# Window attention of a two-block model: the copies of turned probability tiles divided between ScalarE and VectorE by the parity of the unit

## The reference

```python
def softmax_with_sink(s, sink):
    m = jnp.maximum(jnp.max(s, axis=-1, keepdims=True), sink)
    p = jnp.exp(s - m)
    return p / (jnp.sum(p, axis=-1, keepdims=True) + jnp.exp(sink - m))
...
        p = softmax_with_sink(jnp.concatenate([s_lat, s_ctx], axis=-1), sink_f).astype(v.dtype)
        o = jnp.einsum('bhgqk,bkhd->bqhgd', p[..., :3 * BLOCK], vblk)
        return o + jnp.einsum('bhgqc,bchd->bqhgd', p[..., 3 * BLOCK:], vc)
```

## Time and profile before

| what | us |
|---|---|
| median of 3 runs | 2783.05 (2780.53 to 2784.03) |
| the profiled execution, its own time | 2781.07 |
| its span in the profile | 2779.2 |
| TensorE matmul busy in the span | 2627.3 |
| VectorE busy | 1275.1 |
| ScalarE busy | 651.1 |

### The profile page before, as it was taken

How to read it: one execution, slowest core, us unless ns; L and a number is a source line. 1 busy time by engine, 2 the same in 40 slices (tenths; PEclk the granted TensorE clock), 3 DMA queues, 4 the chain that set the end, 5 groups by cost and what they waited for, 6 DMA issues and landing times.

```text
span 2779.2 us, 38625 instructions
## 1 busy us (share of the span) xinstructions
PE 2627.3 (95%) x14448; PEld 2112.1 (76%) x14448; DVE 1275.1 (46%) x1893; ACT 651.1 (23%) x1222; POOL 1355.4 (49%) x880
## 2 busy tenths in 40 slices
PE   7989999999999989889989999999899999899997
PEld 6667777777777767656768888888788887688886
DVE  6941222253222235445454444444486666555555
ACT  2220000031000013567230000000165553211112
POOL 6365555545555563133536344444343425776661
PEclk9999999999999999999989999999999999999998
DMA  5124444434444441100111111111111111222221
GB/s 188 52 77 159 144 143 145 144 113 139 151 146 148 151 137 54 39 1 1 39 39 61 61 60 60 60 58 59 51 37 40 45 46 36 79 91 98 92 97 53
DMA packets 67372, 235.61 MB, mean 85 GB/s; under 512 B 8144, under 2 KB 9552, under 8 KB 67152
## 3 DMA queue, kind: packets, MB, share of 16 engines
q1 hardware_dynamic: 65792, 233.64, 25.5%
q10 hardware_dynamic: 1488, 0.69, 0.1%
HBM read 232.21 MB, written 2.10 MB: 84 GB/s over the span
## 4 chain that ended last, share of the span: by engine, by line
PE 84%; DVE 8%; issue 3%; ACT 2%; POOL 1%; DMA 1%; DVEq 0%; SPq 0%; ACTq 0%; POOLq 0%
PE ps L650 66%; PE ps L1160 2%; PE ps L1183 2%; PE ps L1048 2%; PE ps L843 2%; PE ps L805 2%; PE ps L1122 1%; PE ps L1034 1%; DVE X L2142 1%; PE ps L769 1%; PE ps L1114 1%; DVE Alo L1734 1%; PE ps L683 1%; DVE tmp L1727 1%; DVE X L1745 1%
## 5 line engine op out<-in xcount | busy, mean ns | idle before, releaser
L501 POOL TENSOR_SCALAR whi<-raw 128x1024 fp32r<-128x1024 f32 x332 | 365.6, 1101 | 1060.3 <-DMA raw<-in_stream 1060.0
L503 POOL TENSOR_TENSOR wlo<-raw,whi 128x1024 fp32r<-128x1024 f32 x332 | 808.9, 2437 | 27.7
L650 PE MATMUL ps<-Ahi,whi 128*128 128x512 f32 (+1 forms) x2128 | 730.7, 375 | 39.9 <-DVE Alo L1734 19.3
L650 PE MATMUL ps<-Alo,whi 128*128 128x512 f32 (+1 forms) x2128 | 720.7, 370 | 0.0
L650 PE MATMUL ps<-Ahi,wlo 128*128 128x512 f32 (+1 forms) x2128 | 719.4, 369 | 0.0
L650 PEld LDWEIGHTS ps<-Ahi,whi 128*128 128x128 f32 x2128 | 376.5, 191 | 131.2 <-issue 21.4
L650 PEld LDWEIGHTS ps<-Ahi,wlo 128*128 128x128 f32 x2128 | 375.7, 190 | 68.9
L650 PEld LDWEIGHTS ps<-Alo,whi 128*128 128x128 f32 x2128 | 376.6, 191 | 66.4 <-issue 0.7
L650 PE MATMUL ps<-hhi,whi 128*128 128x512 f32 x1120 | 373.3, 370 | 19.7 <-DVE X L2142 18.6
L650 PE MATMUL ps<-hhi,wlo 128*128 128x512 f32 x1120 | 373.4, 370 | 0.0
L650 PE MATMUL ps<-hlo,whi 128*128 128x512 f32 x1120 | 370.7, 368 | 0.0
(11 more groups left out here) (291 smaller groups left out, 2782.0 us busy)
## 6 DMA issues: line engine op xcount, KB each, us to landing
raw<-in_stream SPq DMA_DIRECT2D x428, 512.0 KB, 3.8
X<-in_xT SPq DMA_DIRECT2D x2, 1024.0 KB, 6.3
arena<-in_dft SPq DMA_DIRECT2D x1, 2048.0 KB, 16.7
out_xT<-X SPq DMA_DIRECT2D x2, 1024.0 KB, 4.3
X<-in_ctxT SPq DMA_DIRECT2D x1, 1024.0 KB, 19.1
w<-in_stream SPq DMA_DIRECT2D x2, 512.0 KB, 4.3
vec<-in_vec SPq DMA_DIRECT2D x1, 364.5 KB, 7.4
arena<-in_fmap SPq DMA_DIRECT2D x1, 256.0 KB, 12.3
```

Of the source, the lines that this page charges most:

```text
L501: pool.tensor_scalar(whi[:, s, part], raw[:, s, part], 1.0, 1.0, ALU.mult, ALU.mult).then_inc(sem("w_hi"), 1)
L503: pool.tensor_tensor(wlo[:, s, part], raw[:, s, part], whi[:, s, part], ALU.subtract).then_inc(sem("w_split"), 1)
L650: mm = pe.matmul(dst[c], w[:, b % RING, off:off + P], rhs(k, part, c0, n), start=(k == 0 and w is whi and part == 0), stop=(k == kn - 1 an ...
```

## The change

`take_turned` is now on two engines. ScalarE copies the turned tiles of even units, VectorE those of odd units, in a function of the same shape. In VectorE's loop the copy stands behind the reciprocal and ahead of `take_values`. The one semaphore `ptA` becomes `ptA0` and `ptA1`, one for each parity, and TensorE's three waits on it are rewritten: ahead of the first turned tile on the copy of the unit two before, ahead of the fifth tile on the copy of the unit one before, and ahead of part 0 of the values on both.

```diff
--- before.py
+++ after.py
@@ -1027,10 +1027,11 @@
 
                 ks = keys(UNITS[u][2])
                 pe.wait_ge(*when("pA", u + 1))
-                pe.wait_ge(*when("ptA", u + 1))
+                if u >= 2:
+                    pe.wait_ge(*when(f"ptA{u % 2}", u // 2))
                 for t in range(len(ks)):
-                    if t == 4:
-                        pe.wait_ge(*when("ptA", u + 2))
+                    if t == 4 and u:
+                        pe.wait_ge(*when(f"ptA{(u - 1) % 2}", (u - 1) // 2 + 1))
                     mm = pe.transpose(turned(u, t), probA[u % 4][:, 1 + t * P:1 + (t + 1) * P], ident[:, :])
                 mm.then_inc(sem("turnA"), 1)
 
@@ -1039,7 +1040,8 @@
                 g, _, n, _ = UNITS[4 * four]
                 ks = keys(n)
                 if part == 0:
-                    pe.wait_ge(*when("ptA", 4 * four + 6))
+                    for parity in range(2):
+                        pe.wait_ge(*when(f"ptA{parity}", 2 * four + 2))
                     pe.wait_ge(*when("oA", four + 1))
                 for t in range(len(ks)):
                     if t // 2 == part:
@@ -1518,7 +1520,6 @@
                 take_query(0, 0, h)
 
 
-            act.sem_inc(sem("ptA"), 2)
             act.sem_inc(sem("sA_free"), 2)
             def take_turned(u):
 
@@ -1531,10 +1532,10 @@
                     copy(ptA[u // 4 % 2][:, 4, h * P:(h + 1) * P], psf[:, 7 * 512:7 * 512 + P])
                     nk = 4
                 copy(ptA[u // 4 % 2][:, 0:nk, h * P:(h + 1) * P],
-                     psf[:, four:four + nk * P].rearrange("p (t q) -> p t q", t=nk)).then_inc(sem("ptA"), 1)
+                     psf[:, four:four + nk * P].rearrange("p (t q) -> p t q", t=nk)).then_inc(sem("ptA0"), 1)
 
             for u in range(N_UNITS + LEAD):
-                if u >= LEAD:
+                if u >= LEAD and (u - LEAD) % 2 == 0:
                     take_turned(u - LEAD)
                 if u < N_UNITS:
                     n = UNITS[u][2]
@@ -2079,6 +2080,19 @@
                 move(O[:, 4 * g + 2 * e:4 * g + 2 * e + 2, n * P:(n + 1) * P],
                      ps[:, 6, 0:2 * P].rearrange("p (a q) -> p a q", a=2)).then_inc(sem("oA"), 1)
 
+            def take_turned(u):
+
+                n, h = UNITS[u][2:]
+                nk = len(keys(n))
+                four = (4 + u % 2) * 512
+                dve.wait_ge(*when("turnA", u + 5))
+                dve.wait_ge(*when("oA_done", u // 4 + 1))
+                if nk > 4:
+                    dve.tensor_copy(ptA[u // 4 % 2][:, 4, h * P:(h + 1) * P], psf[:, 7 * 512:7 * 512 + P])
+                    nk = 4
+                dve.tensor_copy(ptA[u // 4 % 2][:, 0:nk, h * P:(h + 1) * P],
+                     psf[:, four:four + nk * P].rearrange("p (t q) -> p t q", t=nk)).then_inc(sem("ptA1"), 1)
+
             for u in range(N_UNITS + LEAD + 4):
                 if u < N_UNITS:
                     n = UNITS[u][2]
@@ -2095,6 +2109,8 @@
                     c = sm[:, (u - 1) % 8, :]
                     dve.wait_ge(*when("sA_free", u + 2))
                     dve.reciprocal(c[:, 2:3], c[:, 1:2]).then_inc(sem("denA"), 1)
+                if LEAD <= u < N_UNITS + LEAD and (u - LEAD) % 2:
+                    take_turned(u - LEAD)
                 four, part = divmod(u - LEAD - 7, 4)
                 if four >= 0 and part == 0:
                     take_values(four)
```

## The result

The changed kernel takes 2787.65 us (median of 14 runs, 2784.97 to 2791.81), the kernel before 2780.69 in the runs made beside it (14 runs, 2776.84 to 2784.03). The ratio is 1.0027, with a 95% interval from 1.0019 to 1.0035: 5.3 to 9.7 us slower. The time lies in the range and 0.6 us from the forecast; but the forecast stood on a median of before of 2783.05, so the step of 5.1 us was 7.0 in truth. That the two errors, 1.9 us too small a step and a starting point 2.4 us too high, nearly cancel in the time is luck. The likeliest case, a difference too small to tell, was not the one that came: nearly all of the interval is slower by over 0.2%.

A forecast was written before the change was run, and what follows sets the result against it. TensorE was taken to bound the kernel, so only its waits inside the attention count. Late values 4.8 plus fifth tile 0.3 made 5.1 us on 2781.07, plus 1.98 to the median: 2788.2 us, range 2781 to 2792 (8 in 10).

The forecast's parts named there:

- The likeliest case: Whole kernel: a difference from no change within about 0.2%, 5.6 us; chance 0.55, against slower 0.40 and faster 0.05.
- Nothing won on ScalarE's side: TensorE's nine short waits behind exponentials: fewer ScalarE copies gain 0, at most 0.2 us; in four the row maximum was last.
- The rival of relief: ScalarE's halved queue removes short waits if the taking is early enough; at most 3.9 us faster, 2779.2 us; chance 0.18.
- Late values, 4.8 us: Turns that leave 2: VectorE's copy stands ahead of the taking of values, so TensorE's values start late, 4.8 us in all.
- the step from the end of the taking to the values: From VectorE's taking to TensorE's values: 0.05 us for the semaphore, read from ScalarE's copy (1250.11 to 1250.16).
- The fifth tile, 0.3 us in two turns: Turns 17 and 64: the fifth tile, sharing bank 7, waits for VectorE's late copy, about 0.17 us each, together 0.3.
- Row maxima priced at nothing: VectorE's row maxima of odd units come up to 0.8 us later behind the copies; cost to the exponentials priced at 0.
- The seven stalls unchanged: TensorE's seven stalls ended by GpSimd's scaling, 12.0 us in all, behind splittings, were taken as staying unchanged.
- The sum, 5.1 us: Whole kernel: late values 4.8 plus fifth tile 0.3, all else 0, gives 5.1 us slower, with bounds 3.8 to 7.1.
- The signs: Profile after: values of turns 23, 27, 51, 59, 75, 99 wait behind the taking; new row 3 to 5 us, 15 to 19 times.
- signs of being wrong: Stage shorter, VectorE copies under 0.5 us, exponential waits over 1 us longer, or a low clock stretch coming or going.
- The clock as a rival: New 0.38 us gaps behind the stalls of turns 23 and 71 bring low clock stretches, 3.4 us more, 2791.6 us; chance 0.15.

The follow-up runs named there:

- e3_threes: The changed kernel, but VectorE copies only units that leave 3 when divided by 4 (24 of 96), ScalarE all others; 2788.40 us, ratio 1.0017 to before.
- e9: The changed kernel, but ScalarE takes the values out of PSUM, ahead of the exponential; odd units' copies stay on VectorE; 2784.55 us, ratio 1.0016 to before.
- e2_ones: The changed kernel, but VectorE copies only units that leave 1 when divided by 4 (24 of 96), ScalarE all others; 2780.32 us, ratio 1.0000 to before.
- e1_swap: The changed kernel, but VectorE takes the values first and copies the odd unit behind that; 2791.25 us, ratio 1.0041 to before.
- e4: The changed kernel with parities exchanged: VectorE copies even units right behind its row maximum, ahead of the query splitting, ScalarE odd ones; 2774.49 us, ratio 0.9982 to before.
- e7: VectorE order: row maximum, reciprocal, copy of an even unit, splitting, taking of values; ScalarE copies odd units; 2770.17 us, ratio 0.9958 to the kernel before.
- e6: The kernel before, with VectorE's reciprocal ahead of a query's or key's splitting, no copy moved; 2773.08 us, ratio 0.9970 to before.
- e11: Meant to move the taking of values ahead of the splitting in e6, but no instruction moved, so e6 again; 2774.20 us, ratio 0.9983 to before.
- e10: Meant to move the taking of values ahead of the splitting in e7, but no instruction moved, so e7 again; 2770.68 us, ratio 0.9971 to before.
- e12: e7 measured again, unchanged, beside e10 and e11; 2771.22 us, ratio 0.9970 to the kernel before.
- e8: The changed kernel, with VectorE's reciprocal ahead of the splitting; 2787.46 us, ratio 1.0021 to the kernel before.

## Why the prediction was right, and where not

- **Nothing won on ScalarE's side.** Right. The four short waits of turns 10, 34, 58 and 82 still read 0.45 to 0.46 us, and no wait behind an exponential went. The rival of relief is refuted: its condition, a taking that is early enough, fails in 14 turns.
- **Late values, 4.8 us.** Right in place and mechanism: 5.2 us more in the row of waits, 0.64 in turn 51, 0.42 in turn 23, 0.17 in turn 59, 1.21 in place of 0.69 in turn 99. e3_threes puts the loss in the units named, e9 takes the row away. The size was too small in one term. In turn 51 before had a gap of 0.12 us, from the end of its turning (1250.04) to the values (1250.16):

```profile
1249.66 0.38 PE L1034 MATMUL ps<-ident,tmp 128*128 128x128 f32 x2
```

So the delay there is 0.64 - 0.12 = 0.52 us where I worked out 0.40. The copy and the taking took the times that I gave them; the step from the end of the taking to the values did not. I took 0.05 us for it, from ScalarE's copy in the earlier trace rows. Behind VectorE's taking it is 0.15 in all four timelines above (turn 23: 1199.19 + 0.41 = 1199.60, the values at 1199.75). That is some 0.1 us more in each of 17 turns. Counted from the start of the turning ahead of them, the values of these 17 turns come 5.95 us later in all, where I had 4.8, of which 0.3 was for turn 19, where no wait came.
- **The fifth tile, 0.3 us in two turns.** Right: in turn 17 and in the turn that I called 64 (it is 65) the turning takes 0.92 and 0.93 us in place of 0.77. By the trace of before the fifth matmul of turn 65 starts at 1272.7 and each of the five takes 273 to 328 ns; a fifth of 0.77 is 154, so what the prediction calls the drain was 0.12 us.
- **Row maxima priced at nothing.** Too low, by what the list shows: 0.7 us in three more waits behind exponentials, which go with the units that leave 1 (e2_ones has them, e3_threes not).
- **The seven stalls unchanged.** An eighth came, 0.85 us in turn 37, and brought the row to 12.9. It stands where before has a low stretch, behind the stall of turn 35, and after has none; e9, which has this stretch, has 12.0 in 7 again, and e1_swap and e3_threes, which have not, have the eighth stall too. Over the 4 us behind the stall of turn 35 the granted clock was 0.58 in before and 1.00 in after (the earlier trace rows and the third row below). So I read it as the clock's: a TensorE that isn't slowed came to turn 37 with 0.85 us still to wait.
- **The sum, 5.1 us.** It was too small by some 2 us: 5.95 + 0.3 + 0.7 = 6.95 us without the eighth stall, against 7.0 by the medians, whose interval is 5.3 to 9.7. The step that was mis-sized is the 0.05 us from the taking to the values, measured at 0.15; the row maxima, priced at nothing, come second. With it went the bound: at 5.1 the sum lay just below what can be told from no change, and the truth lay just above. The rows of waits give 5.2 + 0.7 + 0.9 = 6.8 us, by another count; the idle time grew by 5.5 only, mainly because the wait at the end of the stage is 0.9 shorter.
- **The signs.** The values of all six turns that I named wait behind the taking; the row came out at 5.9 us in 14 times where I had 3 to 5 in 15 to 19. One of its signs of being wrong did come: low stretches went, two of four between these two profiles. That touches the clock and not the late values, whose waits stand in the trace.
- **The clock as a rival.** Not seen as I described it: behind the 1.72 us stall of turn 23 the granted clock stays at 1.00 with the new gap in it. In the profile after, the first row is the stretch behind the stall of turn 19, the second that of turn 23, the third that of turn 35, where before was low:

```profile
1187.10:1191.10 4.00, 3.98 (x17) 2.08 (x18) 2.21 (x5) 2.97 (x7) 0.76 (x1) 0.57 0.00 0
1198.70:1202.70 4.00, 3.58 (x28) 2.20 (x29) 2.70 (x7) 2.47 (x7) 1.97 (x3) 1.00 0.00 0
1220.20:1224.20 4.00, 3.95 (x30) 2.82 (x30) 2.18 (x6) 2.62 (x6) 0.57 (x1) 1.00 0.00 0
```

- **Open.** One profile of each kernel doesn't tell how often the low stretches come in its other runs. After has two in the middle of the stage, before four, e9 five. The granted clock of whole executions, which every run has, says a little: in the mean 0.9749 in the 14 runs of the change and 0.9748 in 78 runs of before, so the change's loss shows no sign of a lower clock. In the 11 runs of e9 it is 0.9742, against 0.9753 in the 28 beside them, a difference within what such means scatter by. So whether the 4.5 us that e9 keeps are such stretches is not settled; the interval of e9 begins at 1.7 us.

Sharing the copies out of PSUM between ScalarE and VectorE gave a faster kernel in e4 (0.9982) and, by some 3.5 us, in e7 and its repeats beside e6 and e11, and a slower one in the change (1.0027): which pieces go where decided here.

## What to carry to other kernels

Before giving work to the idler engine, look at what else that engine does in the same turn and who waits for both: here two jobs in one queue that release one consumer cost their sum, on an engine that had been busy for half of the stage (90.9 of 184.5 us). The same copies were a loss in the turns of the taking (e3, 1.0017) and none in the others (e2, 1.0000; e4 and e7 even gained), so the half to give away was a matter of place and not of amount. When such delays are added up, the step from the end of one instruction to the start of the one that waits for it should be taken from a row of the same engine: 0.05 us behind ScalarE's copy was 0.15 behind VectorE's taking, in every turn. A splitting that itself waits for another engine should stand behind the short instruction that somebody waits for: the reciprocal moved ahead of it was worth 6 to 9 us alone. Most of the waiting came back at the next instructions behind it (8.5 + 2.4 of 12.0 us in e6), and the profile shows the gain as a TensorE at a higher clock (busy 158.6 us for 165.2, with a mean granted clock in the stage of 0.97 for 0.94), so the idle time alone would not have told it.

## What was not expected of the hardware

The same stalls are followed by low stretches of TensorE's clock in one kernel and not in another: e2_ones has ten stalls behind GpSimd of up to 1.9 us and no low stretch in the middle of the stage, before has seven and four stretches, each at 0.57 or 0.58 over 4 us (the second is in the earlier trace rows). In five of the six profiles without these stalls (e6, e7, e10, e11, e12) there is none; their longest wait in the middle of the stage is 1.6 us. The sixth, e8, has four, with waits behind VectorE of up to 2.3 us, and even there the 2.3 us in turn 23 were followed by none.

Outside of the stage, one execution scatters by more than the effect: e6 and e11 are the same program, with stages of 179.9 and 179.8 us and spans of 2778.3 and 2770.7 us. The length of the stage in one profile told the size of a change better than the span, and wherever the ratio is clear of 1 it agreed with its sign.

VectorE's copies out of PSUM took 676 and 686, 404 and 271 ns in the groups shown, 0.08 to 0.09 us more than ScalarE for 128x512 and about the same for 128x128.

From the end of an instruction to the start of the values on TensorE that it released, these traces show 0.05 us behind ScalarE's copy (before, turns 51 and 99), 0.11 behind VectorE's copy (e9, turn 51) and 0.15 behind VectorE's taking (after, turns 23, 51, 59 and 99).
